# A streaming encoder layer on one core: two of seven block products swapped, row-block sums taken through memory, and loads and first tiles reordered

## The reference

```
z = rms_norm(x) @ w_in                 # u 256 | q 768 | k 192 | v 192
pool_o = pool_mix(u)                   # trailing means over 2/4/8/16 frames, per-group map
attn_o = attention(q, k, v, sinks)     # chunks of 64 frames, 192 keys each, sink logit per head
h = x + concat(pool_o, attn_o) @ w_out
hn = rms_norm(h)
y = h + (silu(hn @ w_gate) * (hn @ w_up)) @ w_down     # width 2816
```

## Time and profile before

| | |
|---|---|
| time, median of 3 runs | 2159.62 us (2154.95 to 2160.76) |
| the profiled execution's own time | 2159.57 us |
| its span, first to last instruction | 2157.8 us |
| busy: TensorE | 2091.9 us, 97% |
| VectorE, ScalarE, GpSimd | 1320.9, 884.7, 797.5 us |
| mean granted clock of TensorE | 0.99 of full speed |
| HBM read, written | 158.50 MB, 35.03 MB |

### The profile page before, as it was taken

How to read it: one execution, slowest core, us unless ns; L and a number is a source line. 1 busy time by engine, 2 the same in 40 slices (tenths; PEclk the granted TensorE clock), 3 DMA queues, 4 the chain that set the end, 5 groups by cost and what they waited for, 6 DMA issues and landing times.

```text
span 2157.8 us, 33524 instructions
## 1 busy us (share of the span) xinstructions
PE 2091.9 (97%) x12454; PEld 1892.5 (88%) x12454; DVE 1320.9 (61%) x2214; ACT 884.7 (41%) x2149; POOL 797.5 (37%) x501
## 2 busy tenths in 40 slices
PE   6999999998999999999999999999999899999998
PEld 6888888876788899999998899999998899999997
DVE  5555656554123466675667866666677766766665
ACT  5666666643334533333333332333333433333331
POOL 1100000033324454444534644354445644444352
PEclk9999999999999999999999999999999999999999
DMA  6111111023675532222123432222223422221221
GB/s 182 30 38 38 41 40 40 23 68 100 216 237 170 166 98 78 79 79 79 60 79 106 166 105 63 78 76 79 79 79 95 162 73 79 79 79 59 79 79 74
DMA packets 236730, 195.59 MB, mean 91 GB/s; under 512 B 20749, under 2 KB 216122, under 8 KB 236570
## 3 DMA queue, kind: packets, MB, share of 16 engines
q1 hardware_dynamic: 236570, 193.46, 29.2%
HBM read 158.50 MB, written 35.03 MB: 90 GB/s over the span
## 4 chain that ended last, share of the span: by engine, by line
PE 88%; DVE 5%; ACT 2%; issue 2%; DMA 1%; POOL 1%; SPq 0%; DVEq 0%; ACTq 0%
PE ps L771 26%; PE ps L773 26%; PE ps L772 25%; PE ps L867 2%; PE ps L841 2%; PE ps L853 1%; PE ps L962 1%; PE ps L785 1%; DVE xs_lo L1485 1%; PE ps L964 1%; PE ps L960 1%; PE ps L829 1%; DVE xs_lo_raw L1480 1%; ACT s_sb L1115 1%; POOL w_lo L688 1%
## 5 line engine op out<-in xcount | busy, mean ns | idle before, releaser
L688 POOL TENSOR_TENSOR w_lo<-w_lo_raw,w_hi 128x512 fp32r<-128x512 f32 (+1 forms) x232 | 388.7, 1681 | 598.7 <-PE ps L773 414.8
L771 PE MATMUL ps<-xs_hi,w_hi 128*128 128x352 f32 x1848 | 597.8, 323 | 10.0 <-issue 5.3
L773 PE MATMUL ps<-xs_lo,w_hi 128*128 128x352 f32 x1848 | 597.9, 324 | 0.0
L771 PEld LDWEIGHTS ps<-xs_hi,w_hi 128*128 128x128 f32 x1848 | 348.0, 188 | 14.1 <-issue 12.6
L1604 DVE TENSOR_TENSOR h<-ps,h 128x512 f32<-128x512 f32 (+1 forms) x396 | 272.1, 689 | 134.4 <-PE ps L773 127.5
L773 PEld LDWEIGHTS ps<-xs_lo,w_hi 128*128 128x128 f32 x1848 | 351.0, 190 | 0.0
L772 PE MATMUL ps<-xs_hi,ws_lo 128*128 128x352 f32 x1056 | 339.5, 322 | 0.0
L688 POOL TENSOR_TENSOR ws_lo<-ws_lo_raw,w_hi 128x512 fp32r<-128x512 f32 x200 | 287.0, 1436 | 120.7 <-DVE ws_lo_raw L1453 76.3
L1182 ACT ACTIVATE w_hi<-ws_lo_raw 128x512 fp32r<-128x512 f32 x264 | 165.6, 627 | 337.2 <-DVE ws_lo_raw L1453 333.1
L771 PE MATMUL ps<-w_hi,act_hi 128*128 128x512 f32 x660 | 259.3, 393 | 10.0 <-issue 9.8
L772 PE MATMUL ps<-w_hi,act_lo 128*128 128x512 f32 x660 | 258.5, 392 | 0.0
(11 more groups left out here) (127 smaller groups left out, 3326.6 us busy)
## 6 DMA issues: line engine op xcount, KB each, us to landing
w_lo_raw<-in_w_gate SPq DMA_DIRECT2D x66, 512.0 KB, 5.1
w_lo_raw<-in_w_up SPq DMA_DIRECT2D x66, 512.0 KB, 5.1
w_lo_raw<-in_w_down SPq DMA_DIRECT2D x66, 512.0 KB, 4.1
xload<-in_x_prompt SPq DMA_DIRECT2D x16, 512.0 KB, 4.5
mix_d<-o_st SPq DMA_DIRECT2D x64, 128.0 KB, 1.8
xt_lo_raw<-mix_d SPq DMA_DIRECT2D x16, 512.0 KB, 6.5
wg_hi_raw<-in_x_prompt SPq DMA_DIRECT2D x16, 512.0 KB, 5.7
h_d<-wg_hi_raw SPq DMA_DIRECT2D x16, 512.0 KB, 2.8
```

The costliest lines, as they stand in the source:

```text
L688: nc.gpsimd.tensor_tensor(lo, raw, hi.bitcast(F32), ALU.subtract).then_inc(done, 1)
L771: nc.tensor.matmul(out, s_hi, m_hi, start=first, stop=False, skip_group_check=partial)
L773: return nc.tensor.matmul(out, s_hi, m_lo, start=False, stop=final, skip_group_check=partial)
```

## The change

Products 4 and 5 trade places, with their weight and row blocks. The one that is a sum of blocks and completes C22 is now product 5 and still adds into the bank of product 2; the plain one, which completes C21, is product 4. C21 so comes ahead of C22, and the first row tiles of the down projection need two low parts (`al_done`) where they needed three. VectorE's queues take the results in the new order, and in an up set the fourth weight sum moves behind the low part.

The row sums of the next part are made during the part before, in its gate sets 2, 4, 5 and 6 (`next_rows_sum`), in two buffers, and stored to memory (`sums_d`); at the part change `load_blocks` brings them and the plain blocks in as each product of the last set lets its buffer go. All seven row lows of a part change are VectorE's. GpSimd's down-weight lows of a part's last group are cut in two, and ScalarE casts those weights ahead of its third gate weight.

Tile 1 is normalised and transposed ahead of tile 0's projection and tile 2 ahead of tile 1's; the first six transposes have banks of their own. GpSimd's split of group 2's weights goes; ScalarE and VectorE split them in steps 2 and 3. The sink logit is a column beside each chunk's scores (`sink_fill`), so that the maximum, the exponential and its sum take it in; `s_sb` rows grow from 384 to 388. SyncE loads x tile 1 ahead of the pool columns, `w_out` parts ahead of a step's stores, and mixed tile 3 at step STEPS - 2. `h_rstd(0)` stands first in its step, and second halves of the later transposes use bank 3. The core of the diff:

```diff
-BANK_OF = (0, 1, 2, 0, 2, 1, 2)
-A_BLOCK = {0: (0, 0), 3: (0, 1), 5: (1, 1)}
+BANK_OF = (0, 1, 2, 0, 1, 2, 2)
+A_BLOCK = {0: (0, 0), 3: (0, 1), 4: (1, 1)}
...
-RESULTS = ((0, 0), (1, 1), (1, 0), (0, 1))
+RESULTS = ((0, 0), (1, 0), (1, 1), (0, 1))
...
-    return 2 + TP[e] % 2 if TP[e] < 6 else 2
+    if TP[e] < 6:
+        return 2 + TP[e]
+    return 3 if e[0] == "x" and e[1] > NTILES and e[2] == 1 else 2
...
+            def next_rows(p, j):
...
+                def store_sum(n, src):
+                    sp.wait_ge(x_sum, 4 * p + n + 1)
+                    sp.dma_start(sums_d[:, p - 1, n], src).then_inc(sums_stored, 16)
+                if j == 1:
...
+                    load(a, rows_block(p, 0, 1), turn_a_loaded)
+                    load(b, rows_block(p, 1, 1), turn_b_loaded)
+                elif j == 2:
+                    store_sum(0, b)
+                elif j == 3:
+                    sp.wait_ge(sums_stored, 16 * (done + 1))
+                    load(b, rows_block(p, 0, 0), turn_b_loaded)
...
+            def load_blocks(p):
+                for m, src in ((2, sums_d[:, p - 1, 2]), (3, rows_block(p, 1, 0)), (4, sums_d[:, p - 1, 3]),
+                               (5, sums_d[:, p - 1, 1]), (6, rows_block(p, 1, 1))):
+                    sp.wait_ge(product_done, after_product(last_set(p), m))
+                    load(xs_raw[:, m], src, block_loaded[m])
...
+            load_x(1)
             load_pool_columns()
-            load_x(1)
             load_group(0)
...
             for n in range(STEPS):
+                for part, unit in enumerate([UNIT[g, SAMPLE] for g in (0, 0, 1)]):
+                    if n == unit + 1:
+                        load_wo(part)
+                if n == STEPS - 2:
+                    load_mixed(3)
                 for e in step_events(n)[1]:
                     if e[0] != "mean":
                         store_mixed(e)
...
-            def low1(G):
+            def low1(G, cuts=1):
                 for c in range(2):
-                    low(w1_high, 2 * G + c + 1, w1_lo[:, c], w1_raw[:, c], w1_hi[:, c], w1_split)
...
+                    for n in range(cuts):
+                        cols = slice(1024 // cuts * n, 1024 // cuts * (n + 1))
+                        low(w1_high, 2 * G + c + 1, w1_lo[:, c, cols], w1_raw[:, c, cols], w1_hi[:, c, cols], w1_split)
...
-            for i in range(2):
-                scale_group(2, i)
-            for i in range(2):
-                wg_low(2, i)
...
-                    low1(G)
+                    low1(G, 2)
                     if p + 1 < PARTS:
                         pool.wait_ge(product_done, after_product(2 * G + 1, PRODUCTS - 1))
-                        for rows, m in ((1, 1), (0, 3), (0, 4), (1, 3), (0, 5), (1, 5), (0, 6)):
...
+                        for m in range(3, PRODUCTS):
+                            low2(2 * G + 2, m)
...
-                    pe.wait_ge((p1_saved, u2_ready, q7_ready, c22_read)[m - 3], s + 1)
+                    pe.wait_ge((p1_saved, q7_ready, u2_ready, c22_read)[m - 3], s + 1)
...
-                    pe.wait_ge(al_done, 4 * G + (3 if PART * (j + 1) <= NB else 4))
+                    pe.wait_ge(al_done, 4 * G + (2 if PART * (j + 1) <= NB else 4))
...
-            for t in range(3):
-                for half in range(2):
-                    x_transposes(t, half)
-                pool_columns(t)
+            for half in range(2):
+                x_transposes(0, half)
+            for half in range(2):
+                x_transposes(1, half)
+            pool_columns(0)
+            for half in range(2):
+                x_transposes(2, half)
+            pool_columns(1)
+            pool_columns(2)
...
+            def sink_fill(n):
...
+                nc.scalar.activation(s_sb[:, n % 3, :, 1:S_ROW:S_ROW - 3][:, :, 0:chunks(t)],
+                                     sink[:, g].unsqueeze(2).to_broadcast([PART, 2, chunks(t)]), ACT.Copy).then_inc(sink_filled, 1)
...
-                nc.scalar.activation(esink[:, b, :, 0:chunks(t)], esink[:, b, :, 0:chunks(t)], ACT.Exp).then_inc(e_ready, 1)
...
             for n in range(STEPS):
+                if n == STEPS - 2:
+                    h_rstd(0)
                 for t in HALF_AT:
...
                 save_p1(s)
+                if s == 0:
+                    stage_copy(NTILES - 1, 0)
...
-                    for m in range(3):
-                        high2(s + 1, m)
+                    high2(s + 1, 0)
+                    high2(s + 1, 1)
+                    if j < GROUPS - 1:
+                        high2(s + 1, 2)
                 high1(G)
+                if j == GROUPS - 1 and G + 1 < NG:
+                    high2(s + 1, 2)
...
-                link(nc.vector.tensor_tensor(top, top, nsink[:, g].unsqueeze(2).to_broadcast([PART, 2, nch]), ALU.min))
...
-                link(nc.vector.tensor_tensor(den[:, b, :, 0:nch], den[:, b, :, 0:nch], esink[:, b, :, 0:nch], ALU.add))
...
+            def next_rows_sum(p, n):
+                a, b = turn_a[:, :, :], turn_b[:, :, :]
...
+                out, other = (b, a) if n % 2 == 0 else (a, b)
+                nc.vector.tensor_tensor(out, out, other, ALU.subtract).then_inc(x_sum, 1)
...
-                m = (4, 5, 6)[n - 1]
+                m = n + 3
                 dve.wait_ge(product_done, after_product(s, m))
-                dve.wait_ge((q7_ready, u2_ready, p1_saved)[n - 1], s + 1)
+                dve.wait_ge((u2_ready, q7_ready, p1_saved)[n - 1], s + 1)
...
-                    .then_inc((c22_read, c21_read, c12_read)[n - 1], 1)
...
+                    .then_inc((c21_read, c22_read, c12_read)[n - 1], 1)
...
                 result_sum(s, 1)
+                result_sum(s, 2)
                 if now:
                     weight_sum(s + 1, 3)
-                result_sum(s, 2)
                 result_sum(s, 3)
+                if p + 1 < PARTS and j in (2, 4, 5, 6):
+                    next_rows_sum(p + 1, (2, 4, 5, 6).index(j))
...
                 low_part(G, 0)
                 act_product(G, 1)
+                result_sum(s, 2)
+                low_part(G, 1)
                 if more:
                     weight_sum(s + 1, 3)
-                result_sum(s, 2)
-                low_part(G, 1)
                 act_product(G, 2)
...
-                        elif p + 1 < PARTS:
-                            rows_sum(p + 1, j)
-                    elif group == GROUPS - 1 and p + 1 < PARTS:
-                        rows_low(p + 1, X_LOWS_DVE[j - 4])
...
+                    elif j > 0 and group == GROUPS - 1 and p + 1 < PARTS:
+                        rows_low(p + 1, j - 1)
```

More of the change, by code:

```diff
@@ L30 @@
 KEYS = 3 * CHUNK
+S_ROW = 2 * KEYS + 4
+S_KEY = 2
+S_CHUNK = KEYS + 1
+NEG = -1e30
 EPS = 1e-6
@@ L296, in build @@
         xs_loaded = sem("xs_loaded")
-        b12_loaded = sem("b12_loaded")
-        b22_loaded = sem("b22_loaded")
-        b11_loaded = sem("b11_loaded")
-        b21_loaded = sem("b21_loaded")
+        turn_a_loaded = sem("turn_a_loaded")
+        turn_b_loaded = sem("turn_b_loaded")
+        block_loaded = [sem(f"block_loaded{m}") for m in range(PRODUCTS)]
         w2_loaded = [sem(f"w2_loaded{i}") for i in range(2)]
@@ L336, in build @@
         nm_ready = sem("nm_ready")
+        sink_filled = sem("sink_filled")
         e_ready = sem("e_ready")
@@ L433, in raw_of @@
                 return w2_raw[s % 2][:, i, j]
-            return ws_raw[:, {1: 0, 2: 1, 4: 2, 6: 3 + s % 2}[m]]
+            return ws_raw[:, {1: 0, 2: 1, 5: 2, 6: 3 + s % 2}[m]]
         def rows_raw(p, m):
-            return b22[:, :, :] if m == 6 and p > 0 else xs_raw[:, m]
+            if p > 0 and m < 2:
+                return (turn_b, turn_a)[m][:, :, :]
+            return xs_raw[:, m]
         def d_index(G, j, nh=0):
@@ L634, in _ @@
                         load_x(t)
-                for part, unit in enumerate([UNIT[g, SAMPLE] for g in (0, 0, 1)]):
-                    if n == unit + 1:
-                        load_wo(part)
                 if NU - 3 <= n < NU:
@@ L670, in _ @@
                     load_down(G)
-                if j == 1 and p + 1 < PARTS:
-                    load_second_halves(p + 1)
-                if j == GROUPS - 1 and p + 1 < PARTS:
-                    load_first_halves(p + 1)
+                if p + 1 < PARTS:
+                    next_rows(p + 1, j)
+                    if j == GROUPS - 1:
+                        load_blocks(p + 1)
                 if j == 0:
@@ L775, in tp_bank @@
             def tp_bank(e):
-                need(pe, tp_free, TP[e] - (TP[e] < 6))
+                if e[0] == "x" and e[1] > NTILES:
+                    pe.wait_ge(tp_free, TP[e] - (e[1] > NTILES + 1 or e[2] == 1))
+                    pe.wait_ge(b3_free, len(B3_EVENTS))
+                elif TP[e] >= 6:
+                    pe.wait_ge(tp_free, TP[e])
                 return ps[:, tp_bank_of(e)]
@@ L1168, in stage_copy @@
                     k = 4 * half + n
```

(16 more changed lines are left out.)

236 lines of the change are left out of this document (114 added, 122 removed).

## The result

The kernel after takes 2195.55 us (median of 4 runs, 2194.23 to 2196.44); the kernel before, run beside it, 2160.19. The ratio over all these runs is 1.0169, 95% interval 1.0151 to 1.0186 (of the two medians alone 1.0164). The forecast was 2186.3, range 2167 to 2214: the sign and the main mechanism came as forecast, the size 8.7 us short (26.7 of 35.4). The profiled execution took 2196.44 us, with a span of 2194.7.

A forecast was written before the change was run, and what follows sets the result against it. TensorE, busy 2091.9 of 2157.8 us, was the bound. 2159.57 + 56.7 (product 6) - 8 (part changes) - 2 (first tiles) - 7 (mixer) - 11 (mixer to output) - 2 (set 0) = 2186.3 us, range 2167 to 2214.

The forecast's parts named there:

- The wait ahead of product 6: Feed forward: TensorE waits for VectorE's bank read in every set, 0.93 us each, 56.7 us over 61 sets.
- so I charge the price in full: Feed forward: VectorE is ready when product 5 ends, so 0.93 us is charged in all sets but five.
- Sets 0 to 2: Start of the feed forward: set 0 wins 2 us, sets 1 and 2 lose 0.93 each; together -0.1.
- Part changes: Two part changes: waits of 3.9 and 2.2 us replace 9.3 a change; 8 us won in all, bounds 0 to 13.
- about 2 us sooner: Part changes: ScalarE casts the down weights earlier, so GpSimd's lows come about 2 us sooner, in four halves.
- Mixer to output: Passage from mixer to output projection: waits and two half-clock stretches go; 11 us won, bounds 5 to 14.
- The mixer's start: First mixer steps: GpSimd's scalings go, shortening a key-copy wait and a half-clock stretch; 7 us won, bounds 2 to 10.
- First tiles: Kernel start: transposing tile 1 earlier removes about 4 us of waits; 2 us won, bounds 0 to 3.
- (b): Product 6: the bank read is covered in every set and the gains come, 2130 us; chance 0.05.
- (d): Feed forward: the clock falls at each new wait, 1.7 us 61 times, 2290 us; chance 0.06.
- (a): Mixer and part changes: the gains stay small, 12 us, giving 2204 us; chance 0.20.
- (c): Whole kernel: no measurable change, gains of 44 against 47.6 us, giving 2163 us; chance 0.07.

The follow-up runs named there:

- experiment 4: Kernel after, with the down projection's first row tile multiplied between products 5 and 6 in gate sets: 2176.32 us, ratio 1.0065.
- experiment 1: Kernel after with products 4 and 5 in their old order, all else as after: 2121.37 us, ratio to before 0.9826.
- experiment 2: Kernel before with the swap of products 4 and 5 alone: 2241.22 us, ratio 1.0381.
- experiment 3: Kernel after, with ScalarE copying product 0 of a gate set ahead of its last cast of the up set before: 2180.91 us, ratio 1.01.
- experiment 9: Old product order in the kernel after, plus down-weight lows in two pieces and their cast behind the third gate weight at part changes: 2125.57 us.
- experiment 8: Kernel after, with ScalarE's first root mean square of the output projection last in its step again: 2199.42 us.
- experiment 7: Kernel after, with four GpSimd multiplications on an otherwise unused buffer where GpSimd scaled group 2's weights before: 2198.61 us.
- experiment 5: Kernel after, with SyncE loading x tile 2 ahead of group 0's weights: 2197.73 us.
- experiment 6: Kernel after with old product order, x tile 2 loaded ahead of group 0's weights and cached keys ahead of the constants: 2125.28 us, ratio 0.9834.

## Why the forecast came out as it did

**The wait ahead of product 6: right, in kind, number and price.** 66 waits, 60 of 0.71 and six of 1.36 to 3.03 in set 0, set 1 and at the part changes; the clock stays full at the short ones; experiment 4 took single ones away for 0.86 to 0.96 each. The idle figure of a row is 0.71, and 66 of them would be 47 us; the remaining 0.22 of each stands in the profile as busy time, and busy time did grow, from 2091.9 to 2102.9, where the forecast had it stay. That the end of a matmul in a profile is an estimate, as the Trainium skill has it (Perfetto Trace Analysis, the part on the Tensor Engine instruction), agrees with this: price such a wait by starts.

**The step that failed: "so I charge the price in full" as the swap's only price.** The forecast followed VectorE's new order up to the sum after product 5 and stopped there; it did not follow it behind product 6, through GpSimd's window, into ScalarE's queue. There a low part that was out of the way before now delays a cast, and the copy behind it: 30 waits, 0.58 each by the groups' starts (44.77 - 42.33 - 2 x 0.93), about 16 us of the 27 groups' 65.8. Experiments 1 and 2 show that the swap makes it; experiment 3, which gave 13.3 of the 16 back, that the place in ScalarE's queue does.

**Sets 0 to 2: the wrong way.** Set 0 was to win 2 and sets 1 and 2 to lose 0.93 each; with the swap the three lost 2.9 up to the first down projection, without it (experiment 1) this stretch takes 38.2 us in place of before's 40.3. The mis-sized term is set 1, charged 0.93: its product 6 waited 2.74, since VectorE's weight sums, which stand ahead, waited 2.61 for a gate weight's load. Behind this wait the clock is at 0.51 from 725.4 to 728.8, which the forecast did not charge either.

```profile
718.19 0.69 DVE L1505 TENSOR_TENSOR ws_lo_raw<-w_lo_raw 128x512 f32<-128x512 f32 x1 [2.61 <-DMA w_lo_raw<-in_w_gate]
...
725.39 0.63 PE L793 MATMUL ps<-xs_hi,w_hi 128*128 128x352 f32 x1 [2.74 <-DVE aa L1562]
```

**Part changes: right in size.** Forecast 3.9 ahead of product 6 and 2.2 in the next set; measured 3.03 and 1.99. The wait ahead of the down projection is gone; at the second change one of 1.04 for VectorE's accumulation stands inside it. The half-clock stretches went from four to three in the two changes. One term of the working is not borne out: GpSimd's lows "about 2 us sooner" saved nothing in experiment 9 (with the old order; with the swap it was not tried). The gain is the change's other parts': with the old order (experiment 1) a change still takes 4.6 to 5.0 less than before.

**Mixer to output: too small by 6.4, the mechanism right.** Of the stretch 437.9 to 727.2 before, 12.4 us were idle, at a mean clock of 0.98; the like stretch after (427.0 to 700.7) has 2.1 idle at 1.00. The forecast counted two half-clock stretches there and half of a long key-copy wait; there were three stretches (experiment 8 shows one come back with its wait), and all but 2.1 us of the waits went. The mixer's middle, charged at nothing, gave 1.8 of the 6.4. The mixer's start, forecast at 7, gave 9.2; experiment 7 shows 5.6 of it to be GpSimd's scalings.

```profile
437.90:727.20 289.30, 276.95 (x1505) 224.52 (x1504) 100.45 (x160) 117.50 (x360) 106.10 (x60) 0.98 0.50 155
```

```profile
427.00:700.70 273.70, 271.57 (x1505) 220.68 (x1503) 91.58 (x133) 117.63 (x359) 107.15 (x60) 1.00 0.53 164
```

**First tiles: the waits did not go.** The forecast had about 4 us of waits removed, down to a floor of 26.9 set by the cached keys' last load. In the kernel after that load is issued at 24.22 and TensorE does not wait for it. It waits for tiles 1 and 2 instead, 1.69 and 3.38: 5.07 us where the kernel before waits 5.94 behind its first transposes (1.90, 1.57, 0.80, 1.67), and the clock is at 0.50 for 6.8 us where before it was for 3.4. Experiments 5 and 6, which take the wait for tile 2 away, show the floor too was low: the cached keys come at 28.65, or a constant at 31.0.

**The rivals.** None came: the read isn't covered (b), the clock doesn't fall at the waits (d), the gains were larger than forecast (39 us by experiment 1, for 30) and not smaller (a), and the interval excludes no change (c).

## What to carry to other kernels

When results change order, ask for each buffer that is added into twice who must read it in between, and keep one independent piece of work, longer than the read and its way back, between the two. Then follow the reader's queue to its end, past the wait that you found: work that is now later there delays the engines that are fed from it, and an instruction that needs none of it may stand behind one that does. In a change of many parts, one part can carry the whole loss: here the parts beside the swap are worth 39 us, and the swap costs 74.

## Of the hardware

At the two part changes of the kernel after the same wait of 3.03 us was followed once by a granted clock of 0.50 and once by 1.00:

```profile
1176.90:1180.30 3.40, 3.39 (x12) 3.40 (x13) 1.55 (x3) 1.49 (x3) 0.00 (x0) 0.50 0.45 182
...
1675.40:1678.80 3.40, 3.32 (x18) 3.14 (x19) 2.67 (x5) 1.57 (x4) 1.07 (x1) 1.00 0.54 211
```

Yet the two changes, from the last down projection ahead of them to the first one in the new part, took 95.7 and 95.6 us: with the clock full, TensorE caught up with VectorE and waited the 1.04 for it. The first change has two half-clock stretches, the second has one. So a half-clock stretch can be free where another engine sets the pace; this was read from the traces, not tried. Nor does the length of a wait alone tell whether the clock falls: in the gate set behind the change product 6 waits 1.99 at the first and 2.00 at the second, and the clock behind it is 1.00 from 1211.1 to 1214.5 and 0.57 from 1707.9 to 1711.3.
